# Row gathers in another order, and row sums and products at other places, in a two-block kernel

## What is computed

```python
def chunk_fn(args):                       # peer(): x + g2 * peer(h2, ...)
    xc, ec, gc = args                     # ec: the expert numbers, gc: their gates
    u = exp_u[ec]
    a = jax.nn.gelu(jnp.einsum('cd,chkd->chk', xc, u).astype(jnp.float32))
    w = (gc * a).astype(exp_v.dtype)
    return jnp.einsum('chk,chkd->cd', w, exp_v[ec])
```

## Time and profile before

| | us |
|---|---|
| median of 3 runs | 3275.3 |
| lowest and highest of them | 3268.85, 3280.11 |
| the profiled execution, its own time | 3277.33 |
| span of that execution | 3275.6 |
| PE busy in it | 3175.5 (97%) |
| DVE busy | 2246.4 (69%) |
| ACT busy | 1259.5 (38%) |
| POOL busy | 370.0 (11%) |
| DMA | 821.57 MB, mean 251 GB/s |

### The profile page before, as it was taken

How to read it: one execution, slowest core, us unless ns; L and a number is a source line. 1 busy time by engine, 2 the same in 40 slices (tenths; PEclk the granted TensorE clock), 3 DMA queues, 4 the chain that set the end, 5 groups by cost and what they waited for, 6 DMA issues and landing times.

```text
span 3275.6 us, 71646 instructions
## 1 busy us (share of the span) xinstructions
PE 3175.5 (97%) x31390; PEld 2833.9 (87%) x31390; DVE 2246.4 (69%) x2685; ACT 1259.5 (38%) x1135; POOL 370.0 (11%) x284
## 2 busy tenths in 40 slices
PE   7999999999999989998989999999999999999998
PEld 4777768899999979988889998888888888888887
DVE  8496145799988766776778776588567765555554
ACT  2000143445544434334434444444443444443332
POOL 0275100000011222221212000300000000000000
PEclk9899999999999999999999999999999999999999
DMA  9657785556688988989788875556555566555553
GB/s 409 258 211 309 296 359 221 181 181 237 215 291 309 367 317 330 322 322 332 314 293 322 309 250 191 199 199 205 192 185 206 179 203 203 196 202 201 198 203 115
DMA packets 105301, 821.57 MB, mean 251 GB/s; under 512 B 12394, under 2 KB 14458, under 8 KB 15552
## 3 DMA queue, kind: packets, MB, share of 16 engines
q1 hardware_dynamic: 86112, 700.49, 59.0%
q0 software_dynamic: 16656, 115.53, 9.3%
q10 hardware_dynamic: 2304, 2.10, 0.2%
HBM read 814.00 MB, written 4.06 MB: 250 GB/s over the span
## 4 chain that ended last, share of the span: by engine, by line
PE 80%; DVE 9%; DMA 8%; issue 2%; ACT 1%; POOL 0%; ACTq 0%; DVEq 0%; SPq 0%; POOLq 0%
PE psW L587 21%; PE psW L589 20%; PE psW L588 20%; PE psW L585 7%; DVE ring L1192 4%; DMA proj<-vrow_dram,rs 3%; DMA arena<-urow_dram,rs 2%; DMA ring<-wst_dram 2%; PE psW L730 1%; PE psM L730 1%; PE psM L659 1%; PE psM L884 1%; PE psM L647 1%; DVE arena L1669 1%; PE psM L587 1%
## 5 line engine op out<-in xcount | busy, mean ns | idle before, releaser
L1192 DVE SCALAR_TENSOR_TENSOR ring<-ring 128x2048 f16<-128x2048 f32 x526 | 1199.9, 2290 | 585.1 <-ACT ring L2033 583.3
L2033 ACT ACTIVATE ring<-ring 128x2048 f16<-128x2048 f32 x526 | 1002.2, 1907 | 959.5 <-PE psW L589 831.0
L587 PE MATMUL psW<-h_act,ring 128*128 128x256 f16 (+1 forms) x5040 | 1337.2, 265 | 11.5 <-DVE ring L1192 6.9
L588 PE MATMUL psW<-h_act,ring 128*128 128x256 f16 (+1 forms) x5040 | 1336.7, 265 | 0.0
L589 PE MATMUL psW<-h_act,ring 128*128 128x256 f16 (+1 forms) x5040 | 1336.4, 265 | 0.0
L587 PE MATMUL psW<-arena,ring 128*128 128x208 f16 (+1 forms) x3072 | 799.2, 260 | 3.3 <-DVE ring L1192 3.3
L588 PE MATMUL psW<-arena,ring 128*128 128x208 f16 (+1 forms) x3072 | 798.9, 260 | 0.0
L589 PE MATMUL psW<-arena,ring 128*128 128x208 f16 (+1 forms) x3072 | 798.8, 260 | 0.0
L587 PEld LDWEIGHTS psW<-h_act,ring 128*128 128x128 f16 x5040 | 494.4, 98 | 72.8 <-issue 20.6
L589 PEld LDWEIGHTS psW<-h_act,ring 128*128 128x128 f16 x5040 | 494.5, 98 | 34.9
L588 PEld LDWEIGHTS psW<-h_act,ring 128*128 128x128 f16 x5040 | 494.4, 98 | 34.2
(11 more groups left out here) (405 smaller groups left out, 2482.4 us busy)
## 6 DMA issues: line engine op xcount, KB each, us to landing
ring<-wst_dram SPq DMA_DIRECT2D x522, 1024.0 KB, 5.2
ring<-wst_dram SPq DMA_DIRECT2D x72, 2048.0 KB, 11.4
proj<-h_rows POOLq DMA_DIRECT2D x6, 1024.0 KB, 19.3
x_res<-xT_dram POOLq DMA_DIRECT2D x2, 2048.0 KB, 17.7
out_dram<-x_res SPq DMA_DIRECT2D x4, 512.0 KB, 2.9
bias_rows<-proj POOLq DMA_DIRECT2D x1, 1536.0 KB, 21.4
x_res<-cmat_dram POOLq DMA_DIRECT2D x1, 1024.0 KB, 5.6
x_res<-bmat_dram ACTq DMA_DIRECT2D x8, 128.0 KB, 3.3
```

What stands on the lines that cost most here:

```text
L587: nc.tensor.matmul(out, whi(s, col, P), xh, start=first, stop=False)
L588: nc.tensor.matmul(out, whi(s, col, P), xl, start=False, stop=False)
L1192: ins = stt(wlo(s, c, n), ring[:, s * UNIT + c:s * UNIT + c + n], WSCALE, whi(s, c, n), ALU.mult, ALU.subtract)
L2033: act(whi(s, p2 * (UNIT // 2), UNIT // 2), ring[:, c], ACT.Copy, scale=WSCALE).then_inc(hi_done, 1)
```

## The change

Six numbers in three functions that lay out the row part. Nothing that is computed changes, and no instruction is added or removed.

```diff
 def dots_at():
-    out, at = [], 22.0
+    out, at = [], 20.0
     for i in range(ROWS_T):
         out.append(int(at))
-        at += 3.0 if i % HEADS == HEADS - 1 else 1.6 if 32 <= at < 96 else 2.1
+        at += 2.8 if i % HEADS == HEADS - 1 else 1.85
...
-        at = max(at + (1.75 if i < ROWS_T - GROUP_T else 1.25), GELU_AT[i // HEADS] + 1)
+        at = max(at + (1.85 if i < ROWS_T - GROUP_T else 1.25), GELU_AT[i // HEADS] + 2)
...
-    u = [(DOT_AT[i - 1] + 0.9 if i else 0.0, "u", i) for i in range(ROWS_T)]
-    v = [(PRODUCT_AT[i - V_BUFS] + 1.0 if i >= V_BUFS else PRODUCT_AT[i] - 3.0, "v", i) for i in range(ROWS_T)]
+    u = [(DOT_AT[i - 1] + 2.2 if i else 0.0, "u", i) for i in range(ROWS_T)]
+    v = [(PRODUCT_AT[i - V_BUFS] + 1.2 if i >= V_BUFS else PRODUCT_AT[i] - 3.0, "v", i) for i in range(ROWS_T)]
```

## The result

The kernel with the change takes 3227.1 us (median of 4 runs, 3224.57 to 3229.0); the kernel before, run beside it, 3273.4 us (3268.85 to 3280.11). The ratio is 0.9857, with a 95% interval of 0.9843 to 0.987: 1.4% faster. The forecast was 3226. The profiled execution took 3224.57 us with a span of 3222.8 us, 52.8 us less than the span before.

What follows compares the result with a forecast made beforehand. PE, busy 97% of the span, was taken as the bound. Profiled execution 3277.3 - 55.8 + 4.5 + 1.5 = 3227.5 us; the median 2.0 lower, 3225.5, stated as 3226; 8-in-10 range 3217 to 3244.

Steps and rivals of the forecast that it cites:

- The 55.8 us: PE from 1100 to 1700 us: 42.8 idle, 4.3 slow products and 8.7 slow units, all expected to go.
- the seven waits: PE, 1100 to 1700 us: five products waiting for `exp_v` gathers (38.45), unit 71 (3.33), product 8 (1.04); 42.82 us in all.
- 4.3 + 8.7: PE's lower-clock loss behind the waits: 4.3 us in five products, 8.7 us in six units.
- Pair 20/21: Dots 0 and 1, one place apart: PE waits 2.2 us at unit 24, up to 4.9 with clock loss; 4.5 taken.
- Dot 32: Its gather u32, behind an `h_load`, has 25.1 us and needs 19.7 to 27.5; cost up to 5, 1.5 us taken.
- the end: `add_rows` at place 124 instead of 121; DVE catches up at 127, just in time: nothing, at most 2 us.
- the weights set the pace: Slower rival: ACT's 55.2 us of waits for weights reach PE, 72 us with clock, 3291; slower than 3285 had 0.04.
- u8: At this `h_load` PE did not wait although ACT did; cited against the slower rival, no cost put down.
- `gelu + 2`: Weights' due place moved from gelu + 1: product 8's wait of 1.04 us goes; no other group waited.
- the spacing of the dots: Dot 25 two places behind dot 24: unit 71's 3.33 us wait and its share of 8.7 us go.
- The cause: Gathers come late by POOL's fixed issue order, behind `h_load` or two u gathers, not for want of a free buffer.
- The load: DMA traffic in the middle: 331 GB/s against 322 before, share rising from 0.87 to about 0.9.

Runs made afterwards that it cites:

- e2: The changed kernel with only the two offsets of the gathers' sort put back, dots and products at the new places; 3254.0 us, ratio 0.9947.
- e7: The changed kernel with dot 1 at place 22 instead of 21 and nothing else moved; 3222.7 us, ratio 0.9851.
- e3: The changed kernel with gathers v9, v25 and v33 put back behind the `h_load` and its u gather; 3231.7 us, one run.
- e8: The changed kernel with only the products' rule put back (1.75 apart, gelu + 1), new gather order and dots kept; 3233.1 us, ratio 0.9877.
- e1: The kernel before with only the two offsets of the gathers' sort changed, dots and products at old places; 3240.0 us, ratio 0.9899.
- e5: The kernel before with only the first `h_load` kept, so groups 1 to 5 use group 0's vectors; 3229.7 us, one run.
- e9: The kernel before with the five later `h_load`s reading 1 MB from 128 different rows of `exp_u`; 3230.3 us, ratio 0.986.
- e11: The kernel before with vectors written 16 times to DRAM in six 1 MB writes, so `h_load` reads 128 distinct rows; 3254.7 us, ratio 0.9931.
- e10: The changed kernel with vectors written 16 times to DRAM in six 1 MB writes from 8 partitions, read as distinct rows; 3242.6 us, ratio 0.9892.
- e12: The changed kernel with 16 copies of the vectors in DRAM, written as sixteen 384 KB transfers from 48 partitions over ten units; 3216.1 us, ratio 0.983.

## Why the prediction was right

**The 55.8 us.** All three parts were there: the seven waits went, and the products and units behind them run at full speed again. Windows of the expert layer in before and in after:

```profile
706.41:1971.41 1265.00, 1215.18 (x14416) 1159.09 (x14414) 994.63 (x1106) 560.56 (x403) 204.90 (x104) 0.98 0.82 299
...
706.82:1918.66 1211.84, 1201.84 (x14417) 1152.82 (x14415) 993.60 (x1106) 559.25 (x403) 197.02 (x104) 1.00 0.85 313
```

PE's idle time fell from 49.8 to 10.0 us, by 39.8 = 42.8 - 3.0, where 3.0 us is what PE waits newly; its busy time fell by 13.3 us, where 4.3 + 8.7 = 13.0 was put down. This step held because the seven waits were all the idle time of the stretch and each was followed to its cause.

**The last microsecond is luck.** The forecast for the profiled execution was 3227.5 us and it took 3224.57, because the new waits were put at 6.0 us and came to 3.0. The median was then put 2.0 us below that execution, as before; this time it lies 2.6 us above, since the profiled execution is the fastest of the four. The two errors nearly cancel, and so 3226 meets 3227.1.

**Pair 20/21.** Foreseen: PE waits 2.2 us at unit 24, with clock loss 4.5. Measured: 1.85 us and no clock loss; the unit behind it took 8.56 us. But the loss is real in other kernels with the same dots. PE alone, the 96 matmuls of unit 24 in after and in e2, where it waited 2.12 us:

```profile
937.82:946.38 8.56, 8.56 (x96) 1.00 0.87 322
...
936.08:946.30 10.22, 10.22 (x96) 0.83 0.90 348
```

So the term was 2.7 us too large for this execution; with the wait of e2 it would have been 3.8 us in all, within the forecast's 4.9.

**Dot 32.** Its gather landed 21.4 us after it was issued, inside the limit of 25.1. DVE waited 6.95 us and PE nothing; 1.5 was put down. For the end the forecast had nothing to 2 us; PE's only wait there is 0.2 us, as before.

**Not foreseen: 1.14 us at unit 101**, where the weights were late behind the last `h_load`. It is the place where the rival "the weights set the pace" came true, at 1.1 of the 55.2 us it feared. From 1100 to 1700 us ACT waits more than before (68.4 us in 25 waits) but never longer than 7.3 us at a time, against 12.3. The forecast took u8 for safe; units 37 and 38 in e7 and unit 38 in e3 show that it is not by much.

**`gelu + 2`** was under-priced as a part, though not in the sum: 1.04 us in the old trace; once the gathers are in time the products' rule takes away 7.4 us of such waits (e8). In the same way the spacing of the dots hid more than its 3.33 us, since unit 85 would have waited 4.79 (e1). The old trace shows a wait only where no earlier one covers it. The sum came out right since the full change treats all of them; for either part alone this step would have failed, and my expectations for e1 and e2 did.

**The cause.** "Not for want of a free buffer, but by POOL's fixed order" is half of it. The order is a true lever (e1), yet the old order costs 8.3 us of waits for gathers once `h_load` reads nothing (e5) and 9.3 once it reads distinct rows (e9), against 38.45; in e11, which computes the same output, 9.2. The root is the transfer that the forecast only noted in passing ("the transfers then crawl"). The new order and the new places make room for it.

**The load** came to 340 GB/s at a share of 0.91; 331 and 0.9 were forecast. The Trainium skill, page "DMA: Bandwidth & Descriptors", section "Specifications", gives about 358 GB/s as a core's limit to HBM. It is no ceiling in this kernel, with one core at work: in e10 the 20 us from 1196 to 1216 read

```profile
DMA packets 1163, 8.43 MB, mean 422 GB/s; under 512 B 136, under 2 KB 136, under 8 KB 136
```

a mean of 422 GB/s with gathers, weights and an `h_load` of distinct rows at once.

## What to carry to other kernels

When several waits lie in a row on the engine that bounds, price them together: taking one away uncovers the next, so undo parts of a change in both directions before saying what each is worth. When a queue's transfers are late behind a certain one, look at how that one reads before moving everything around it: the five repeated reads cost the old kernel 43.6 us of its expert layer, where the whole reordering won 53.2. And a repair has a price at its own place: the copies' writes cost e10 18.4 us, and in e12, smaller, from more partitions and at another pace, nothing that can be told.

## What the runs showed of the hardware

- A transfer of 1 MB that reads 8 rows of 8 KB sixteen times each landed in 15.7 to 23.5 us in before; 1 MB from 128 distinct rows took 7.1 to 9.1 us (medians of e12, e10, e11 and e9). While the repeated one runs, all queues together move 234 instead of 419 GB/s (after, 1184.5 to 1200 and 1172 to 1180 us) with the DMA engines equally busy, and an 8 KB packet of the weights takes 532 instead of 309 ns.
- Writes of 1 MB to DRAM from 8 partitions took 28.6 us each (median, up to three at once), and their 8 KB packets 1105 ns, while the weights' packets beside them kept 309 ns (e10, 795 to 866 us). Writes of 384 KB from 48 partitions took 6.4 us, with packets of 309 ns in the median (e12).
- A short wait of PE may cost clock or not. No loss: 1.85 and 1.14 us in after (the units behind took 8.56 us), 2.69 us in e5 (the product behind it took 1.06 us). Loss: 2.12 us in e2 (the unit took 10.22 us), 2.00 us in e5 (the product took 1.92 us), 3.33 us in before (11.23 us). The length of the wait alone does not decide it.
- All DMA together held 422 GB/s over 20 us, with this one core at work.
